# Four feed-forward stages: a 512-column product takes both parts of the operand with the high weights

## The chip, the cores and the metric

The kernel runs on one NeuronCore of one Trainium2 chip. Five engines work side by side, each with its own instruction list: TensorE (PE in the profile; its weight loads are shown apart as PEld), VectorE (DVE), ScalarE (ACT), GpSimd (POOL) and SyncE (SP, which here only issues DMAs). They meet through semaphores. The metric is the device time of one execution in microseconds, and lower is better. Both kernels of this document compute the same function.

## What is computed

The reference is two transformer blocks on 256 tokens with a model width of 1024. The change lies in the feed-forward parts, of which there are four: two with a causal three-tap convolution, and two without it.

```python
def conv_ffn(h, w_up, conv_w, conv_b, w_down):      # stages 0 and 1
    u = h @ w_up                                    # 256x1024 @ 1024x5632
    u = conv(u, conv_w, padding=[(2, 0)], per channel) + conv_b
    a, b = u[..., :D_FF], u[..., D_FF:]             # D_FF = 2816
    return (silu(a) * b) @ w_down                   # 256x2816 @ 2816x1024

def _swiglu(x, w_in, w_out):                        # stages 2 and 3
    gate, up = split(x @ w_in, 2)
    return (silu(gate) * up) @ w_out
```

Each follows `rms_norm(x) * gain`. Around them stand the mixers (a gated linear recurrence, latent attention, memory attention, a convolution with gated linear attention) and an output gate; the change touches none of these.

## The kernel before

**Two parts for every float32 operand.** TensorE multiplies fp32r numbers. For accuracy each operand is split: `w_hi` is the weight rounded to fp32r, `w_lo` the rest, and the activations become `h_hi` and `h_lo` in the same way. `three` (lines 351 to 354) then issues three matmuls into one PSUM region: high by high, high by low, low by high.

**The weight stream.** All weights come as units of 128 x 3072 floats through three slots (`raw`). ScalarE makes `w_hi` of each third of a unit (`hi`, L983), VectorE makes `w_lo` (`lo`, L1502), 1024 columns at a time.

**A feed-forward stage** goes through 22 chunks of 128 hidden channels (`CH = 22`). On TensorE a chunk is `up(j)` and `down(j)`. `up(j)` computes the two halves z = 0 (a) and z = 1 (b) of the chunk: for each half eight contraction steps k, each of them a `three` with 256 columns. Both halves lie side by side in one PSUM bank, `4 + j % 3`, so three chunks are in flight. `down(j)` multiplies the 128 gated channels by the rows of w_down: 12 matmuls of 512 columns into banks 0 to 3, which hold the stage's sum throughout. TensorE's order in the loop is up(j), down(j-2), up(j+1), down(j-1), and so on.

**The evacuation of a chunk** (`body` of ScalarE and of VectorE). VectorE multiplies both halves from PSUM by `rb`, the row factors of the norm, into `tu` (L1604) and signals `tu_done` for each half. In stages 0 and 1 ScalarE starts the convolution (L1078) and VectorE adds the two other taps (L1618). Then come the silu (ScalarE, L1083 or L1086), the product of the halves (VectorE, L1648), and the split of it into `y_hi` and `y_lo` (L983, L1651). Between these steps each engine splits the weights of later units. Instructions of one engine run strictly in the order in which they are written.

**The start of a stage.** `first_up` does chunk 0 while the normed operand still arrives. `spread` then builds the row factors in bank 7 from `late_factors`, ScalarE copies them to `rb`, and TensorE goes on with up(1), up(2), down(0) without a word from VectorE: the only waits of `up` are those for the weights (`s_lo`). Before VectorE's body of chunk 0 stand three weight splits (L1502).

**The end of a stage.** `last_downs` does chunks 20 and 21, and waits with `last_lo_done` for the first half of chunk 21's gated channels; that half comes from the chain tu, convolution, silu, product, y_hi, y_lo (L1604, L1078, L1618, L1083, L1638, L1641).

The names `chain` and `dve_chain` stand for a semaphore on which VectorE waits for results of its own.

Of the kernel before, what the change touches and what calls it, by code (L numbers as in the profile page):

```python
# [17 lines left out]
F32R = mybir.dt.float32r  # L18
# [7 lines left out]
P = 128  # L26
# [105 lines left out]
def build(nc, stream, vectors, masks, x_in, mem_in, pos_in, ple_in, fin_in, out):  # L132
    with ExitStack() as ctx:
# [11 lines left out]
        w_hi = sb("w_hi", [P, SLOTS, UNIT], F32R)  # L145
        w_lo = sb("w_lo", [P, SLOTS, UNIT], F32R)
        x = sb("x", [P, T, D])
        h_hi = sb("h_hi", [P, KT, S], F32R)
        h_lo = sb("h_lo", [P, KT, S], F32R)
        y_hi = sb("y_hi", [P, KT, S], F32R)  # L150
        y_lo = sb("y_lo", [P, KT, S], F32R)
        mem_k = sb("mem_k", [P, 2, 2, S])
# [20 lines left out]
        def A(at, *shape):  # L173
            return room(arena, at, shape)
# [63 lines left out]
        go, gosq = A(0, T, 512), A(1024, T * G_HEADS, P)  # L238
        g_abs = A(8056, T, 256)

        cv, sa, gg, tu = A(0, 3, 512), A(1536, 3, S), A(2304, 3, S), A(6144, 3, 512)

        fin, proj, sg = A(4096, D), A(5120, T, D), A(0, T, D)
# [4 lines left out]
        FFNS = ((U_FFN0, "cw0"), (U_FFN1, "cw1"), (U_FFN2, None), (U_FFN3, None))  # L248
        UP0 = (0, CH, None, None)
        FFN_NORM = (1, 3, 4, 6)  # L250

# [92 lines left out]
        def _(pe):  # L346
# [114 lines left out]
            def ffn(i):  # L461
# [5 lines left out]
                def up_part(j, z, k):  # L467
                    s, a = (U0 + j) % SLOTS, slice(z * PIECE + k * P, z * PIECE + k * P + P)
                    return three(ps[:, 4 + j % 3, z * S:(z + 1) * S], w_hi[:, s, a], w_lo[:, s, a],
                                 h_hi[:, k, :], h_lo[:, k, :], k == 0, k == KT - 1)  # L470

                def up(r, j):
                    for z in range(2):
                        pe.wait_ge(s_lo, lo_at(r, j, z))
                        for k in range(KT):
                            m = up_part(j, z, k)
                    m.then_inc(sem("up_ready"), 1)

                def first_up():
# [499 lines left out]
        def _(act):  # L979
# [83 lines left out]
            def ffn(i):  # L1063
                (U0, cw), n0 = FFNS[i], i * CH

                def at(r, n, per=3):
                    return n if r is None else r * per + n

                def body(r, j):
                    g = j % 3  # L1070
                    if cw:
                        a = _cols[cw][0] + 8 * j

                        def w(n):
                            return vec[:, a + n:a + n + 1] if r is None else vec[:, bass.ds(r * 24 + (a + n), 1)]
                        for z in range(2):
                            act.wait_ge(sem("tu_done"), at(r, 2 * (n0 + j) + z + 1, 6))
                            act.activation(cv[:, g, z * S:(z + 1) * S], tu[:, g, z * S:(z + 1) * S], ACT.Identity,  # L1078
                                           scale=w(4 * z + 2), bias=w(4 * z + 3)).then_inc(sem("ev_done"), 1)
                        if r is not None or j < CH - 1:  # L1080
                            hi(r, U0 + j + 2, 1)
                        act.wait_ge(sem("conv_done"), at(r, n0 + j + 1))
                        act.activation(sa[:, g, :], cv[:, g, 0:S], ACT.Silu).then_inc(sem("silu_done"), 1)  # L1083
                    else:
                        act.wait_ge(sem("tu_done"), at(r, 2 * (n0 + j) + 1, 6))
                        act.activation(sa[:, g, :], tu[:, g, 0:S], ACT.Silu).then_inc(sem("silu_done"), 1)  # L1086
                        if r is not None or j < CH - 1:
                            hi(r, U0 + j + 2, 1)
                    if r is not None or j < CH - 1:
                        hi(r, U0 + j + 2, 2)  # L1090
                    if r is None and j == CH - 1:
                        act.wait_ge(sem("last_gate_done"), i + 1)
                        copy(y_hi[:, g, 0:P], gg[:, g, 0:P]).then_inc(sem("last_hi_done"), 1)
                        act.wait_ge(sem("gate_done"), n0 + CH)
                        copy(y_hi[:, g, P:S], gg[:, g, P:S]).then_inc(sem("g_hi_done"), 1)
                        hi(None, U0 + j + 2, 2)
                        hi(None, U0 + j + 3, 0, up_done=True)
                        return
                    act.wait_ge(sem("gate_done"), at(r, n0 + j + 1))
                    copy(y_hi[:, g, :], gg[:, g, :]).then_inc(sem("g_hi_done"), 1)  # L1100
                    hi(r, U0 + j + 3, 0, up_done=True)
                    if r is None and j == CH - 2:
                        hi(None, U0 + j + 3, 1)

                hi(None, U0 + 2, 0)
                spread(FFN_NORM[i])
                body(None, 0)
                with act.Fori(0, (CH - 1) // 3 - 1) as r:
                    for j in range(1, 4):
                        body(r, j)  # L1110
                for j in range(CH - 3, CH):
                    body(None, j)
# [373 lines left out]
        def _(dve):  # L1486
# [107 lines left out]
            def ffn(i):  # L1594
# [5 lines left out]
                def body(r, j):  # L1600
                    b, g = 4 + j % 3, j % 3
                    dve.wait_ge(sem("up_ready"), at(r, n0 + j + 1))
                    for z in range(2):
                        dve.tensor_tensor(tu[:, g, z * S:(z + 1) * S], ps[:, b, z * S:(z + 1) * S], rb,  # L1604
                                          ALU.mult).then_inc(sem("tu_done"), 1)
                    if cw:
                        marks = []
                        for tap in (1, 0):
# [48 lines left out]
                dve.wait_ge(sem("rb_done"), i + 1)  # L1657
                body(None, 0)
                with dve.Fori(0, (CH - 1) // 3 - 1) as r:
                    chain.enter(r, 9 if cw else 0)  # L1660
                    for j in range(1, 4):
                        body(r, j)
                    chain.leave((CH - 1) // 3 - 1)
# [663 lines left out]
```

## Time and profile before

| | |
|---|---|
| median of 3 runs | 1225.86 us (1224.70 to 1229.43) |
| the profiled execution | 1226.63 us, of which its span is 1224.8 us |
| TensorE matmul busy | 1192.5 us, 8139 matmuls |
| weight loads busy | 1105.2 us |
| VectorE busy | 894.2 us (73%) |
| ScalarE busy | 682.8 us (56%) |
| granted TensorE clock, mean | 0.99 of full |
| DMA | 211.48 MB, mean 173 GB/s |

The profiled execution's time is the span plus 1.83 us around it. A busy TensorE isn't necessarily one at its peak, since matmuls overlap: of two neighbours, start to start is what one costs. The rows below give starts in us from the start of the span. A long uninterrupted stretch of TensorE starts can therefore be counted, and the gaps in it are what other engines cost.

### The profile page before, as it was taken

How to read it: one execution, taken by the hardware profiler on the slowest of the kernel's cores; microseconds unless marked ns; L12 is line 12 of the kernel's file. 1: busy time of each engine (PE TensorE's matmuls, PEld its weight loads, DVE VectorE, ACT ScalarE, POOL GpSimd, SP SyncE). 2: the span in 40 equal slices, each digit the busy share in tenths (PEclk: the TensorE clock that was granted, in tenths of full speed). 3: DMA queues.
4: the chain of work that ended last, by engine and by line, in shares of the span. 5: the costliest groups of instructions: out<-in, count | busy, mean ns of one | idle time of the engine just before them, and what ended most of it. 6: DMA issues, size and time to landing. Idle time of an engine off the chain costs nothing.

```text
span 1224.8 us, 21613 instructions
## 1 busy us (share of the span) xinstructions
PE 1192.5 (97%) x8139; PEld 1105.2 (90%) x8140; DVE 894.2 (73%) x1712; ACT 682.8 (56%) x1206; POOL 3.5 (0%) x9
## 2 busy tenths in 40 slices
PE   9999999999999789999999999999999999999997
PEld 7989979999999667999999999999899889999985
DVE  6987878978778765897877765565789667556566
ACT  6954556655556763665554644443557655444454
POOL 0000000000000000000000000000000000000000
PEclk9999999999999999999999999999999999999998
DMA  9543333554555313365454455545354046554540
GB/s 349 204 177 140 119 138 139 222 193 169 202 181 212 123 53 155 142 220 194 168 203 180 180 214 197 183 176 204 140 184 166 30 165 236 191 191 169 205 155 35
DMA packets 21303, 211.48 MB, mean 173 GB/s; under 512 B 2624, under 2 KB 2880, under 8 KB 4480
## 3 DMA queue, kind: packets, MB, share of 16 engines
q1 hardware_dynamic: 20880, 208.90, 46.3%
q0 software_dynamic: 368, 1.84, 0.4%
q8 instruction: 36, 0.59, 0.2%
q14 instruction: 19, 0.16, 0.0%
HBM read 209.68 MB, written 1.05 MB: 172 GB/s over the span
## 4 chain that ended last, share of the span: by engine, by line
PE 92%; DVE 4%; ACT 3%; issue 1%; POOL 0%; ACTq 0%; POOLq 0%
PE ps L352 28%; PE ps L353 27%; PE ps L354 27%; PE ps L357 8%; ACT arena L983 1%; PE ps L449 1%; DVE h_lo L1584 1%; DVE x L1573 1%; DVE w_lo L1502 1%; ACT w_hi L983 0%; PE ps L593 0%; PE ps L783 0%; DVE arena L1861 0%; DVE arena L1810 0%; DVE arena L1812 0%
## 5 line engine op out<-in xcount | busy, mean ns | idle before, releaser
L1502 DVE TENSOR_TENSOR w_lo<-raw,w_hi 128x1024 fp32r<-128x1024 f32 (+1 forms) x390 | 448.5, 1168 | 71.5 <-ACT w_hi L983 71.2
L352 PE MATMUL ps<-h_hi,w_hi 128*128 128x256 f32 x1608 | 455.8, 283 | 0.0
L353 PE MATMUL ps<-h_lo,w_hi 128*128 128x256 f32 x1608 | 455.0, 283 | 0.0
L354 PE MATMUL ps<-h_hi,w_lo 128*128 128x256 f32 x1608 | 455.0, 283 | 0.0
L983 ACT ACTIVATE w_hi<-raw 128x1024 fp32r<-128x1024 f32 (+1 forms) x390 | 382.9, 1009 | 52.2 <-PE ps L354 48.3
L353 PEld LDWEIGHTS ps<-h_lo,w_hi 128*128 128x128 f32 x1608 | 308.3, 192 | 3.2
L352 PEld LDWEIGHTS ps<-h_hi,w_hi 128*128 128x128 f32 x1608 | 308.3, 192 | 3.2
L354 PEld LDWEIGHTS ps<-h_hi,w_lo 128*128 128x128 f32 x1608 | 308.3, 192 | 0.0
L352 PE MATMUL ps<-w_hi,y_hi 128*128 128x512 f32 (+2 forms) x550 | 211.4, 384 | 1.1 <-DVE y_lo L1872 1.0
L353 PE MATMUL ps<-w_lo,y_hi 128*128 128x512 f32 (+2 forms) x550 | 209.0, 380 | 0.0
L354 PE MATMUL ps<-w_hi,y_lo 128*128 128x512 f32 (+2 forms) x550 | 208.1, 378 | 0.0
L1604 DVE TENSOR_TENSOR arena<-ps,arena 128x256 f32<-128x256 f32 x176 | 66.4, 419 | 108.8 <-PE ps L354 108.8
L352 PEld LDWEIGHTS ps<-w_hi,y_hi 128*128 128x128 f32 x550 | 104.0, 189 | 18.9 <-issue 2.0
L354 PEld LDWEIGHTS ps<-w_hi,y_lo 128*128 128x128 f32 x550 | 103.6, 188 | 19.1
L353 PEld LDWEIGHTS ps<-w_lo,y_hi 128*128 128x128 f32 x550 | 104.0, 189 | 14.7
L1078 ACT ACTIVATE arena<-arena,vec 128x256 f32<-128x256 f32 x88 | 48.2, 594 | 120.3 <-DVE arena L1604 120.3
L1086 ACT ACTIVATE arena<-arena 128x256 f32<-128x256 f32 x44 | 18.4, 418 | 154.0 <-DVE arena L1604 154.0
L1618 DVE SCALAR_TENSOR_TENSOR arena<-arena,vec 128x254 f32<-128x254 f32 (+1 forms) x176 | 77.2, 481 | 25.4 <-ACT arena L1078 25.1
L357 PE MATMUL ps<-arena 128*128 128x64 f32 (+4 forms) x484 | 72.7, 305 | 12.2 <-ACT arena L983 9.5
L357 PEld LDWEIGHTS ps<-arena 128*128 128x128 f32 (+2 forms) x484 | 64.3, 194 | 18.9 <-ACT arena L983 11.0
L352 PE MATMUL ps<-w_hi,h_hi 128*128 128x384 f32 (+3 forms) x208 | 70.1, 337 | 0.0
L354 PE MATMUL ps<-w_hi,h_lo 128*128 128x384 f32 (+3 forms) x208 | 68.8, 331 | 0.0
(272 smaller groups left out, 980.2 us busy)
## 6 DMA issues: line engine op xcount, KB each, us to landing
raw<-in_stream SPq DMA_DIRECT2D x129, 1536.0 KB, 6.5
raw<-in_stream SPq DMA_DIRECT2D x3, 512.0 KB, 6.8
x<-in_x SPq DMA_DIRECT2D x2, 512.0 KB, 4.8
arena<-in_mem SPq DMA_DIRECT2D x1, 1024.0 KB, 13.4
x<-in_x POOLq DMA_DIRECT2D x1, 1024.0 KB, 5.3
out<-arena SPq DMA_DIRECT2D x4, 256.0 KB, 2.1
vec<-in_vectors SPq DMA_DIRECT2D x1, 633.0 KB, 8.1
arena<-in_final POOLq DMA_DIRECT2D x1, 512.0 KB, 3.8
```

Of the source, the lines that this page charges most:

```text
L352: pe.matmul(o, lh, rh, start=start, stop=False, skip_group_check=True)
L353: pe.matmul(o, lh, rl, start=False, stop=False, skip_group_check=True)
L354: return pe.matmul(o, ll, rh, start=False, stop=stop, skip_group_check=True)
L357: return pe.matmul(o, l, r, start=start, stop=stop, skip_group_check=True)
L449: m = pe.transpose(ps[:, XT_BANK[k % 4], (k // 4) * S + t * P:(k // 4) * S + (t + 1) * P], x[:, t, k * P:(k + 1) * P], ident)
L983: return act.activation(o, i, ACT.Copy, scale=scale)
L1078: act.activation(cv[:, g, z * S:(z + 1) * S], tu[:, g, z * S:(z + 1) * S], ACT.Identity, scale=w(4 * z + 2), bias=w(4 * z + 3)).then_inc(s ...
L1086: act.activation(sa[:, g, :], tu[:, g, 0:S], ACT.Silu).then_inc(sem("silu_done"), 1)
L1502: dve.tensor_tensor(w_lo[:, s, a], raw[:, s, a], w_hi[:, s, a], ALU.subtract).then_inc(s_lo, 1)
L1573: dve.scalar_tensor_tensor(x[:, t, r], ps[:, 2 * t + half, :], scale, x[:, t, r], ALU.mult, ALU.add).then_inc(sem("x_done"), 1)
L1604: dve.tensor_tensor(tu[:, g, z * S:(z + 1) * S], ps[:, b, z * S:(z + 1) * S], rb, ALU.mult).then_inc(sem("tu_done"), 1)
L1618: m = dve.scalar_tensor_tensor(c, tu[:, g, z * S:(z + 1) * S - d], w, c, ALU.mult, ALU.add)
```

## The change

Eight rows k of the operand's two parts now lie side by side, so that `h_both[:, k]` is one run of 512 columns. In chunks 1 to 21 of all four stages a step k of a half is no longer three matmuls of 256 columns but two: 512 columns (both parts by `w_hi`), and 256 columns (`h_hi` by `w_lo`) on top of the first half of the result. The sum of a half is then in two pieces that lie in one bank, and someone has to add them: ScalarE copies the second piece to SBUF (`second`), VectorE adds the two from PSUM and SBUF into `tu`, and multiplies by `rb` in place. A half now fills a bank, so the three banks hold three halves and no longer three chunks (`half_bank`), and TensorE waits for `tu_done` ahead of each half. Chunk 0 is computed and evacuated as before.

```diff
+        h_both = sb("h_both", [P, KT, 2, S], F32R)
+        h_hi, h_lo = h_both[:, :, 0, :], h_both[:, :, 1, :]
...
+        def second(i):
+            return cv if FFNS[i][1] is None else A(7680, 3, 512)
...
+        BOTH = (0, 1, 2, 3)
+
+        def half_bank(j, z):
+            return 4 + (2 * j + z + 2) % 3
+
+        def part_at(r, i, j):
+            n = BOTH.index(i) * (CH - 1) + j
+            return n if r is None else r * 3 + n
...
+                def up_both(j, z):
+                    s, b = (U0 + j) % SLOTS, half_bank(j, z)
+                    for k in range(KT):
+                        a = slice(z * PIECE + k * P, z * PIECE + k * P + P)
+                        full(ps[:, b, :], w_hi[:, s, a], h_both[:, k, :, :].rearrange("p a b -> p (a b)"), k == 0, k == KT - 1)
+                        m = full(ps[:, b, 0:S], w_lo[:, s, a], h_hi[:, k, :], False, k == KT - 1)
+                    return m
+
                 def up(r, j):
                     for z in range(2):
                         pe.wait_ge(s_lo, lo_at(r, j, z))
-                        for k in range(KT):
-                            m = up_part(j, z, k)
+                        if i in BOTH:
+
+                            n = max(2 * j + z - 3, 1) + 1 + 2 * n0
+                            pe.wait_ge(sem("tu_done"), n if r is None else r * 6 + n)
+                            m = up_both(j, z)
...
+                        if i in BOTH and (r is not None or j > 0):
+                            act.wait_ge(sem("up_ready"), at(r, n0 + j + 1))
+                            for z in range(2):
+                                m = copy(second(i)[:, g, z * S:(z + 1) * S], ps[:, half_bank(j, z), S:2 * S])
+                            m.then_inc(sem("part_done"), 1)
...
                     dve.wait_ge(sem("up_ready"), at(r, n0 + j + 1))
-                    for z in range(2):
-                        dve.tensor_tensor(tu[:, g, z * S:(z + 1) * S], ps[:, b, z * S:(z + 1) * S], rb,
-                                          ALU.mult).then_inc(sem("tu_done"), 1)
+                    if i in BOTH and (r is not None or j > 0):
+                        sums = []
+                        dve.wait_ge(sem("part_done"), part_at(r, i, j))
+                        for z in range(2):
+                            sums.append(chain.inc(dve.tensor_tensor(tu[:, g, z * S:(z + 1) * S],
+                                                                    ps[:, half_bank(j, z), 0:S],
+                                                                    second(i)[:, g, z * S:(z + 1) * S], ALU.add)))
+                        for z in range(2):
+                            dve.wait_ge(s_chain, chain.at(sums[z]))
+                            v = tu[:, g, z * S:(z + 1) * S]
+                            dve.tensor_tensor(v, v, rb, ALU.mult).then_inc(sem("tu_done"), 1)
```

The copies stand in both branches of ScalarE's `body`. In stages 2 and 3 its second weight piece, `hi(r, U0 + j + 2, 1)`, moves from behind the silu to behind the copies.

The order of instructions changes at two places of interest. The first is TensorE at the start of stage 0, where `spread` (the two rows with `vec,small`) ends and up(1) begins. Before:

```order
L357 MATMUL ps<-zero 128x1 [waits lo_ready]
L357 MATMUL ps<-vec,small 128x128 [waits late_factors]
L357 MATMUL ps<-vec,small 128x128
L352 MATMUL ps<-h_hi,w_hi 128x256 [waits lo_ready]
L353 MATMUL ps<-h_lo,w_hi 128x256
```

And now, where L372 is the matmul of `full`:

```order
L372 MATMUL ps<-zero 128x1 [waits lo_ready]
L372 MATMUL ps<-vec,small 128x128 [waits late_factors]
L372 MATMUL ps<-vec,small 128x128
L372 MATMUL ps<-h_both,w_hi 128x512 [waits tu_done,lo_ready]
L372 MATMUL ps<-h_both,w_lo 128x256
```

The first matmul of up(1) now waits for `tu_done` too; the number is 2, which is both halves of chunk 0. The second place is VectorE's evacuation of a chunk in the loop of stage 0. Before:

```order
L1604 TENSOR_TENSOR arena<-ps,arena 128x256 [waits up_ready]
L1604 TENSOR_TENSOR arena<-ps,arena 128x256
L1615 ISA
L1618 ISA [waits ev_done]
L1618 SCALAR_TENSOR_TENSOR arena<-arena,vec 128x255
```

Now, with the sums (L1649) and the products (L1655):

```order
L1647 REGISTER_ALU [waits up_ready]
L1649 TENSOR_TENSOR arena<-ps,arena 128x256 [waits part_done]
L1649 TENSOR_TENSOR arena<-ps,arena 128x256
L1653 ISA
L1655 TENSOR_TENSOR arena<-arena 128x256 [waits dve_chain]
L1653 REGISTER_ALU
L1655 TENSOR_TENSOR arena<-arena 128x256 [waits dve_chain]
L1669 ISA
```

Two vector instructions have become four, the first behind a wait for ScalarE, the last two behind waits for VectorE's own sums.

## Rows read from the trace of the kernel before

**Rows 1.** The page: busy time, the chain that ended last.
```profile
PE 1192.5 (97%) x8139; PEld 1105.2 (90%) x8140; DVE 894.2 (73%) x1712; ACT 682.8 (56%) x1206; POOL 3.5 (0%) x9
...
PE 92%; DVE 4%; ACT 3%; issue 1%; POOL 0%; ACTq 0%; POOLq 0%
```

**Rows 2.** Timeline (start us, us, what) of TensorE, a steady chunk of stage 0.
```profile
231.00 0.40 PE L352 MATMUL ps<-w_hi,y_hi 128*128 128x512 f32 x1
...
233.75 0.28 PE L352 MATMUL ps<-h_hi,w_hi 128*128 128x256 f32 x1
...
239.50 0.40 PE L352 MATMUL ps<-w_hi,y_hi 128*128 128x512 f32 x1
```

**Rows 3.** Timeline of TensorE: other widths, full clock.
```profile
80.06 0.33 PE L353 MATMUL ps<-w_lo,h_hi 128*128 128x384 f32 x1
80.23 0.33 PE L354 MATMUL ps<-w_hi,h_lo 128*128 128x384 f32 x1
...
867.50 0.39 PE L352 MATMUL ps<-w_hi,y_hi 128*128 128x512 f32 x1
...
871.36 0.39 PE L354 MATMUL ps<-w_hi,y_lo 128*128 128x512 f32 x1
```

**Rows 4.** Timeline of VectorE, one chunk of stage 0, the start before and the next.
```profile
232.84 0.75 DVE L1604 TENSOR_TENSOR arena<-ps,arena 128x256 f32<-128x256 f32 x2
...
239.99 0.75 DVE L1604 TENSOR_TENSOR arena<-ps,arena 128x256 f32<-128x256 f32 x2
241.33 1.77 DVE L1618 SCALAR_TENSOR_TENSOR arena<-arena,vec 128x255 f32<-128x255 f32 x4 [0.59 <-ACT arena L1078]
...
244.15 0.42 DVE L1648 TENSOR_TENSOR arena<-arena 128x256 f32<-128x256 f32 x1
244.49 1.22 DVE L1502 TENSOR_TENSOR w_lo<-raw,w_hi 128x1024 fp32r<-128x1024 f32 x1
...
248.20 0.76 DVE L1604 TENSOR_TENSOR arena<-ps,arena 128x256 f32<-128x256 f32 x2 [0.97 <-PE ps L354]
```

**Rows 5.** Timeline, start of stage 0: spread, up(1), ScalarE's copy, VectorE.
```profile
193.47 0.69 PE L357 MATMUL ps<-vec,small 128*128 128x128 f32 x4
193.91 0.36 PE L352 MATMUL ps<-h_hi,w_hi 128*128 128x256 f32 x1
...
194.19 0.39 ACT L983 ACTIVATE arena<-ps 128x256 f32<-128x256 f32 x1 [0.69 <-PE ps L357]
...
196.23 0.75 DVE L1604 TENSOR_TENSOR arena<-ps,arena 128x256 f32<-128x256 f32 x2
...
204.04 0.75 DVE L1604 TENSOR_TENSOR arena<-ps,arena 128x256 f32<-128x256 f32 x2
```

**Rows 6.** Timeline, start of stage 3: up(1) and VectorE's chunk 0.
```profile
1004.52 0.36 PE L352 MATMUL ps<-h_hi,w_hi 128*128 128x256 f32 x1
...
1006.84 0.75 DVE L1604 TENSOR_TENSOR arena<-ps,arena 128x256 f32<-128x256 f32 x2
```

**Rows 7.** Timeline, end of stage 0: the chain of chunk 21, and TensorE.
```profile
367.20 0.76 DVE L1604 TENSOR_TENSOR arena<-ps,arena 128x256 f32<-128x256 f32 x2 [0.77 <-PE ps L354]
...
370.89 0.29 DVE L1641 TENSOR_TENSOR y_lo<-arena,y_hi 128x128 fp32r<-128x128 f32 x1 [0.18 <-ACT y_hi L983]
...
370.88 0.39 PE L354 MATMUL ps<-w_hi,y_lo 128*128 128x512 f32 x1
371.33 0.47 PE L352 MATMUL ps<-w_hi,y_hi 128*128 128x512 f32 x1
```

**Rows 8.** Timeline of VectorE, end of stage 2.
```profile
865.25 0.29 DVE L1641 TENSOR_TENSOR y_lo<-arena,y_hi 128x128 fp32r<-128x128 f32 x1 [0.17 <-ACT y_hi L983]
```

**Rows 9.** Windows: busy us of PE, PEld, DVE, ACT, POOL, granted clock, DMA.
```profile
145.10:155.00 9.90, 9.23 (x68) 8.96 (x69) 7.00 (x30) 4.78 (x27) 0.44 (x1) 1.00 0.15 62
...
460.80:464.20 3.40, 2.90 (x8) 2.43 (x9) 2.71 (x5) 0.57 (x2) 0.00 (x0) 0.50 0.10 22
```

**Rows 10.** Timeline of TensorE: idle time before, and matmuls at half clock.
```profile
145.02 2.16 PE L357 MATMUL ps<-x,arena 128*128 128x128 f32 x17 [1.08 <-DVE arena L1835]
...
459.37 0.55 PE L812 MATMUL ps<-vec,arena 128*128 128x128 f32 x3 [2.49 <-DVE arena L1999]
...
463.17 0.63 PE L353 MATMUL ps<-w_lo,y_hi 128*128 128x512 f32 x1
463.60 0.63 PE L354 MATMUL ps<-w_hi,y_lo 128*128 128x512 f32 x1
```

More of the change, by code:

```diff
@@ L474, in up @@
                         pe.wait_ge(s_lo, lo_at(r, j, z))
-                        for k in range(KT):
-                            m = up_part(j, z, k)
+                        if i in BOTH:
+                            n = max(2 * j + z - 3, 1) + 1 + 2 * n0
+                            pe.wait_ge(sem("tu_done"), n if r is None else r * 6 + n)
+                            m = up_both(j, z)
+                        else:
+                            for k in range(KT):
+                                m = up_part(j, z, k)
                     m.then_inc(sem("up_ready"), 1)
@@ L1084, in body @@
                     else:
+                        both = i in BOTH and (r is not None or j > 0)
+                        if both:
+                            act.wait_ge(sem("up_ready"), at(r, n0 + j + 1))
+                            for z in range(2):
+                                m = copy(second(i)[:, g, z * S:(z + 1) * S], ps[:, half_bank(j, z), S:2 * S])
+                            m.then_inc(sem("part_done"), 1)
+                            if r is not None or j < CH - 1:
+                                hi(r, U0 + j + 2, 1)
                         act.wait_ge(sem("tu_done"), at(r, 2 * (n0 + j) + 1, 6))
                         act.activation(sa[:, g, :], tu[:, g, 0:S], ACT.Silu).then_inc(sem("silu_done"), 1)
-                        if r is not None or j < CH - 1:
+                        if not both and (r is not None or j < CH - 1):
                             hi(r, U0 + j + 2, 1)
@@ L1602, in body @@
                     dve.wait_ge(sem("up_ready"), at(r, n0 + j + 1))
-                    for z in range(2):
-                        dve.tensor_tensor(tu[:, g, z * S:(z + 1) * S], ps[:, b, z * S:(z + 1) * S], rb,
-                                          ALU.mult).then_inc(sem("tu_done"), 1)
+                    if i in BOTH and (r is not None or j > 0):
[5 more added lines that the diff above has]
+                                                                    second(i)[:, g, z * S:(z + 1) * S], ALU.add)))
+                        for z in range(2):
+                            dve.wait_ge(s_chain, chain.at(sums[z]))
+                            v = tu[:, g, z * S:(z + 1) * S]
+                            dve.tensor_tensor(v, v, rb, ALU.mult).then_inc(sem("tu_done"), 1)
+                    else:
+                        for z in range(2):
+                            dve.tensor_tensor(tu[:, g, z * S:(z + 1) * S], ps[:, b, z * S:(z + 1) * S], rb,
+                                              ALU.mult).then_inc(sem("tu_done"), 1)
                     if cw:
@@ L1659, in ffn @@
                 with dve.Fori(0, (CH - 1) // 3 - 1) as r:
-                    chain.enter(r, 9 if cw else 0)
+                    chain.enter(r, (9 if cw else 0) + (6 if i in BOTH else 0))
                     for j in range(1, 4):
```

2 lines of the change are left out of this document (removed).

## The prediction, made before the changed kernel was run

> **What bounds the kernel now.** I read the page first. Matmuls are busy for 97% of the span and TensorE makes 92% of the chain that ended last [rows 1], so what counts is how long TensorE takes over its list, and every time it stands still. Next the timeline of TensorE over one steady chunk, because a busy TensorE says nothing of its pace. From the first matmul of one down to the first of the next is 239.50 - 231.00 = 8.50 us [rows 2]. Of that, the down's 12 matmuls of 512 columns take 2.75 us (0.229 each), and the up's 48 of 256 columns take 5.75 us (0.120 each). Then the timeline of VectorE, which has the next longest list: when it is behind, a chunk costs it 239.99 - 232.84 = 7.15 us, in which it idles 0.59 us for ScalarE; once it has caught up it idles 0.97 us and more for TensorE [rows 4]. Last, the two ends of a stage, where TensorE could come to wait.
>
> **What the change removes.** Per step k of a half, three matmuls of 256 become one of 512 and one of 256. The columns stay the same, 768; one instruction pair (load and matmul) goes. What is a pair worth? Full clock is 2.4 GHz, so 256 columns stream in 106.7 ns and 512 in 213.3. Start to start it is 120 ns for 256 [rows 2], 170 for 384 (160 streamed), and 3.86 us / 17 = 227 for 512 [rows 3]. So about 13 ns come on top of the streaming, whatever the width. Before a step costs 3 x 120 = 360 ns, after it 227 + 120 = 347. 21 chunks x 4 stages x 16 steps = 1344 steps x 13 ns = **17.5 us** saved. With the down's 229 instead of 227 it is 11 ns, 14.8 us. The round falls from 8.50 to 8.29 us. How a 512 and a 256 alternate the trace doesn't show; the nearest rows are those of each alone, and I take 13 ns with 10 and 26 as ends (26 if the short one lost its whole surplus because its load lies behind the long one).
>
> The Trainium skill ("TensorE: Matmul & The Clock Gate", Back-to-back issue gap) gives an isolated matmul a gap of N / 2.4 + 2.5 ns. By that rule a pair removed would be worth an estimated 2.5 ns, 1344 of them 3.4 us, and the sum would be +16.5 us. The trace does not agree: its three widths show 10 to 14 ns above streaming [rows 2, 3].
>
> **What it adds within a chunk.** ScalarE gets two copies of 128x256 from PSUM. One such copy takes 0.39 us [rows 5], the pair about 0.72. VectorE gets two more operations of 128x256. The two PSUM products take 0.75 us as a pair; an SBUF one costs 244.49 - 244.15 = 0.34 start to start [rows 4]. So four take 0.75 + 0.68 and the body grows by 0.7 us, to 7.15 + 0.7 = 7.85 us. A wait of VectorE on its own first sum is covered by the second sum. 7.85 is below the new 8.29, so VectorE doesn't become the bound of the round: cover 0.44 us. The lower end of the addition is the 0.68 of two more SBUF operations; the upper has ScalarE's copies exposed in every round, 0.68 + 0.77 = 1.45, a body of 8.60, which exceeds 8.29 by 0.31. I take 0.7, because a VectorE that is behind finds the copies done.
>
> The new wait for a bank: the second half of up(j+1) needs the first half of chunk j evacuated. Between the end of up(j) and that point TensorE has a down (2.74) and a half of up (2.78), 5.5 us. The evacuation takes 0.77 (copies and a signal) + 0.69 (sums) + 0.41 = 1.9 us. Hidden, with 3.6 us of cover in the steady state. At up(2) of the start there is no down between, only 2.78 us, and VectorE still has chunk 0's body to finish; worked through below it is met with some 0.3 us to spare. Behind the waiting matmul stands all of TensorE's list, so whatever is not covered counts in full.
>
> **The start of a stage.** This is what speaks against the change. Up(1) used to begin straight behind spread, at 193.91 us in stage 0 [rows 5]. Now its first half waits for `tu_done` 2 + 2 n0, both halves of chunk 0, though it writes banks that chunk 0 doesn't use. VectorE produces them only after three weight splits: 196.23 + 0.75 = 196.98 [rows 5]. Plus some 0.1 us for the signal (371.18 to 371.33 is 0.15 [rows 7]), TensorE stands for 197.1 - 193.91 = 3.2 us. In stage 3 it is 1006.84 + 0.75 + 0.1 - 1004.52 = 3.2 us [rows 6]; stages 1 and 2 have the same lists. Nothing covers it, since TensorE is the bound from there on: 4 x 3.2 = **12.8 us** lost. For up(2): up(1) then ends at 197.1 + 16 x 0.347 = 202.65, the copies are done by 203.7, VectorE comes free at 204.04 [rows 5], its first half is done at 204.04 + 0.69 + 0.41 = 205.15, and TensorE asks at 202.65 + 2.78 = 205.4. No stall, by 0.3 us. The later chunks gain 0.44 us of distance per round.
>
> **The end of a stage.** In stage 0 the chain of chunk 21 starts at 367.20 and delivers at 370.89 + 0.29 = 371.18, and TensorE takes it up at 371.33, 0.45 us behind its last start instead of 0.23, so already late [rows 7]. The chain grows by the copies, 0.77, and the sums, 0.69: 1.46 us, all of it exposed. Two convolution stages: **2.9 us**. In stage 2 the chain delivers at 865.54 [rows 8] and TensorE needs it at 867.50 [rows 3], 1.96 us later; there and in stage 3 the 1.46 is covered.
>
> **The clock.** An idle TensorE can lose its clock. After 2.49 us of idle time [rows 10] came 3.4 us at a granted 0.50, which is 1.2 of 2.4 GHz [rows 9]; after 1.08 us at 145.02 the clock stayed at 1.00 [rows 9, 10]. At half clock 512 columns take 463.60 - 463.17 = 0.43 us instead of 0.227 [rows 10, 3]. In dense work such a stretch loses 3.4 x (1 - 0.227 / 0.43) = 1.6 us. My stalls of 3.2 us are nearer the 2.49 than the 1.08, but they sit in dense work. I take the price as between 0 and 4 x 1.6 = 6.4 us, and choose 70% of it at 1.5 us each, since part of a stretch may fall into the stall: **4.2 us**.
>
> **The sum** against the profiled execution's own 1226.63 us: -17.5 + 12.8 + 2.9 + 4.2 = +2.4, that is 1229.0. That execution is 0.8 us above the median of the runs, so on their scale I forecast 1225.9 + 2.4 = **1228 us**: what the shorter list brings is spent at the starts of the stages. With the ends of the terms: -17.5 + 12.8 + 2.9 + 0 = -1.8 (1224), and -14.8 + 12.8 + 2.9 + 6.4 = +7.3 (1233).
>
> **The rivals.**
> - *The short matmul runs faster behind the long one.* Its load hides behind 213 ns of streaming, and the step costs 334. For it: in the all-256 stretch a load has only 120 ns to hide in. Against it: in the all-512 stretch the load is hidden just as well and the surplus of 13 ns is still there. Saving 26 x 1344 = 35 us: 1226 - 35 + 12.8 + 2.9 + 4.2 = 1211; with half of the extra, 1219. Chance 0.12.
> - *A pair is worth next to nothing* (slower): the surplus isn't paid per instruction but comes back in the mixed stream, say as a wait of the 512 for the load that has only 120 ns of the short one to hide in. Then the step stays at 360 ns and only the costs are left: 1226 + 12.8 + 2.9 + 4.2 = 1246. Against it: a load hidden behind 256 columns is what all of the up has now, at 13 ns. Chance 0.03. The gap rule of the Trainium skill's page named above points the same way.
> - *VectorE becomes the bound of the convolution stages (slower).* The place is the body of chunks 1 to 21 of stages 0 and 1; it decides from a body of 8.29 us on, where mine has 7.85. At 8.60 some 40 rounds cost 0.31 us more each, 12 us: 1240; half way over the edge, 8.45, it is 6 us: 1234. For it: VectorE's margin is the smallest in the kernel, and the copy needs ScalarE first. Against: its 0.97 us of idle time, of which only 0.21 go with the shorter round. Chance 0.10.
> - *The clock falls at every start, and for two stretches* (slower): 4 x 3.2 = 12.8 instead of 4.2: 1237. For it: a stall of 3.2 us may reach into parts of two stretches. Against: the only stretch behind a single gap in the rows is one of 3.4 us. Chance 0.12.
>
> **How the numbers follow.** The main forecast has 0.63, with a range of its own from 1224 to 1233. About what a measurement here can tell from no change is 0.5%, which is 6.1 us: below 1219.7 is faster, above 1232.0 slower. Faster is the first rival, 0.12. Slower are the second, third and most of the fourth, and a sliver of the main case: 0.22. The same is left with 0.66. The range, 1221 to 1236, holds the main case, part of the fourth rival and the milder half of the third, and leaves out the faster rival and the dear ends.
>
> **What would show it.** In the changed profile: a step k of 0.347 us start to start, and rounds of 8.29 us between first downs. At each of four stage starts an idle time of about 3.2 us of TensorE, released by VectorE's second product of chunk 0, and behind most of them a granted clock of 0.50 for 3.4 us. At 371 us, less what was shifted, a TensorE gap 1.5 us longer than before in stages 0 and 1, none in 2 and 3. In the convolution stages VectorE still idle before its sums. The prediction fails if the step costs under 0.340 us or VectorE has no idle time left there.

## The result, and the profile after

| | before | after |
|---|---|---|
| median of the runs | 1227.64 us (4 runs) | 1239.22 us (4 runs, 1238.13 to 1242.98) |
| ratio after / before | | 1.0092, 95% interval 1.0069 to 1.0116 |
| profiled execution, span | 1224.8 us | 1236.9 us |
| matmuls | 8139 | 6796 |

The kernel became slower by 0.9%, some 11 us, where 1228 and "no change" were forecast, with a range that ended at 1236. 1343 matmuls are gone, as they should be. The page after (section 1, then section 4, the chain that ended last), against [rows 1]:

```profile
PE 1189.7 (96%) x6796; PEld 1039.1 (84%) x6796; DVE 947.3 (77%) x1880; ACT 736.8 (60%) x1374; POOL 3.5 (0%) x9
...
PE 87%; DVE 8%; ACT 3%; issue 1%; DMA 0%; SPq 0%; DVEq 0%; ACTq 0%
```

TensorE's share of the chain fell from 92 to 87% and VectorE's doubled from 4 to 8%: TensorE now stands and waits for VectorE. The view of who waited for whom (total us, times, longest) names where:

```profile
PE ps L372 <- DVE arena L1658: 11.9, 4, 3.0
...
PE ps L367 <- DVE y_lo L1695: 3.0, 2, 1.5
```

L1658 is the product of chunk 0 with `rb`, once in each of four stages. L1695 is the last chunk's `y_lo`, once in each of stages 0 and 1. Neither row is among the waits of the kernel before.

**A round.** The timeline of TensorE over the round that answers to [rows 2], from the first matmul of one down to that of the next:

```profile
242.00 0.40 PE L367 MATMUL ps<-w_hi,y_hi 128*128 128x512 f32 x1
...
244.75 0.39 PE L372 MATMUL ps<-h_both,w_hi 128*128 128x512 f32 x1
244.97 0.28 PE L372 MATMUL ps<-h_both,w_lo 128*128 128x256 f32 x1
245.09 0.40 PE L372 MATMUL ps<-h_both,w_hi 128*128 128x512 f32 x1
245.32 0.28 PE L372 MATMUL ps<-h_both,w_lo 128*128 128x256 f32 x1
245.44 0.40 PE L372 MATMUL ps<-h_both,w_hi 128*128 128x512 f32 x1
245.68 0.28 PE L372 MATMUL ps<-h_both,w_lo 128*128 128x256 f32 x1
245.80 0.40 PE L372 MATMUL ps<-h_both,w_hi 128*128 128x512 f32 x1
...
250.39 0.40 PE L367 MATMUL ps<-w_hi,y_hi 128*128 128x512 f32 x1
```

The round takes 250.39 - 242.00 = 8.39 us and not 8.29, and nothing in it stands. The up's 16 steps take 250.39 - 244.75 = 5.64 us, 352.5 ns each where 347 were forecast: the 512 that follows a 256 costs 0.23 to 0.24 (mean 0.236) and not 0.227, and the 256 behind it 0.117.

**VectorE in a round**, against [rows 4]:

```profile
249.65 1.22 DVE L1544 TENSOR_TENSOR w_lo<-raw,w_hi 128x1024 fp32r<-128x1024 f32 x1
251.28 0.76 DVE L1649 TENSOR_TENSOR arena<-ps,arena 128x256 f32<-128x256 f32 x2 [0.41 <-ACT arena L1012]
251.95 0.75 DVE L1655 TENSOR_TENSOR arena<-arena 128x256 f32<-128x256 f32 x2
253.39 1.75 DVE L1672 SCALAR_TENSOR_TENSOR arena<-arena,vec 128x255 f32<-128x255 f32 x4 [0.69 <-ACT arena L1112]
```

It still idles 0.41 us before its sums, where 0.97 stood. It isn't the bound.

**The start of a stage**, against [rows 5] (timeline of TensorE, stage 0):

```profile
191.87 0.69 PE L372 MATMUL ps<-vec,small 128*128 128x128 f32 x4
195.52 0.56 PE L372 MATMUL ps<-h_both,w_hi 128*128 128x512 f32 x1 [2.96 <-DVE arena L1658]
...
196.73 0.63 PE L372 MATMUL ps<-h_both,w_hi 128*128 128x512 f32 x1
197.15 0.42 PE L372 MATMUL ps<-h_both,w_lo 128*128 128x256 f32 x1
197.37 0.63 PE L372 MATMUL ps<-h_both,w_hi 128*128 128x512 f32 x1
...
199.24 0.39 PE L372 MATMUL ps<-h_both,w_hi 128*128 128x512 f32 x1
199.47 0.28 PE L372 MATMUL ps<-h_both,w_lo 128*128 128x256 f32 x1
```

After 2.96 us of idle time up(1) begins, and at first a step takes 197.37 - 196.73 = 0.64 us instead of 0.35. The windows behind three of the starts (stages 0, 1, 2; busy us of each engine, then the granted clock, the DMA share and GB/s) say why:

```profile
195.80:199.20 3.40, 3.40 (x12) 2.84 (x11) 3.06 (x6) 3.37 (x5) 0.00 (x0) 0.50 0.88 372
...
506.40:513.20 6.80, 5.97 (x19) 5.13 (x20) 5.66 (x12) 5.94 (x8) 0.00 (x0) 0.50 0.63 233
702.40:709.00 6.60, 6.55 (x37) 5.75 (x38) 4.22 (x5) 3.92 (x8) 0.00 (x0) 1.00 0.74 284
```

Half clock for 3.4 us in stage 0 and for 6.8 us in stage 1, none in stage 2 after the same standing, and 3.4 us in stage 3. A granted clock of 0.50 is 1.2 of 2.4 GHz.

**The end of stage 0**, against [rows 7]:

```profile
371.68 0.39 PE L369 MATMUL ps<-w_hi,y_lo 128*128 128x512 f32 x1
373.55 0.47 PE L367 MATMUL ps<-w_hi,y_hi 128*128 128x512 f32 x1 [1.48 <-DVE y_lo L1695]
```

The gap from start to start grew from 0.45 to 1.87 us.

**The bill**, from starts of TensorE's list in the two traces. The mark is the one-column matmul at the end of `first_up`; from it to the first down it took 12.07 us in every stage before, and 16.59, 17.75, 15.08 and 16.44 us after, in which 3.21 us are standing (from the mark to up(1) it is 3.70 instead of 0.49) and 0.23 are saved in two ups (in the bill, that 0.23 is part of the shorter rounds).

| term | forecast | measured |
|---|---|---|
| shorter rounds, 84 chunks | -17.5 | 84 x (8.387 - 8.500) = -9.5 |
| standing at four starts | +12.8 | 4 x 3.21 = +12.8 |
| half clock behind the starts | +4.2 | 1.54 + 2.70 + 0.03 + 1.39 = +5.7 |
| two late ends | +2.9 | 2 x 1.42 = +2.8 |
| everything outside the feed-forward stages | 0 | +0.2 |
| sum | +2.4 | +12.0 (spans: +12.1) |

The +0.2 is luck and not calm. Ahead of stage 0 the changed kernel was 1.6 us faster, and a stretch of 3.4 us of half clock at 75.1 us in the trace before is absent from its own; in the mixer between stages 0 and 1 it was 1.7 us slower, with 20.5 us of half clock in all instead of 13.7. No edit touches either place. With one traced execution of each kernel, terms of 1 to 2 us outside the stages can't be put down to the change.

### The profile page after: what moved, and what is told of

It is laid out like the page before. It is cut to its first block, busy times and chain, and to the rows that moved or that the text cites. A ratio compares the mean times of both kernels' runs of the same rounds, so it can differ in the third digit from the quotient of the medians.

```text
span 1236.9 us, 19658 instructions
## 1 busy us (share of the span) xinstructions
PE 1189.7 (96%) x6796; PEld 1039.1 (84%) x6796; DVE 947.3 (77%) x1880; ACT 736.8 (60%) x1374; POOL 3.5 (0%) x9
## 4 chain that ended last, share of the span: by engine, by line
PE 87%; DVE 8%; ACT 3%; issue 1%; DMA 0%; SPq 0%; DVEq 0%; ACTq 0%
PE ps L372 45%; PE ps L367 13%; PE ps L368 13%; PE ps L369 13%; DVE w_lo L1544 2%; DVE h_both L1626 1%; ACT arena L1012 1%; PE ps L464 1%; ACT w_hi L1012 1%; DVE x L1615 1%; DMA x<-in_x 0%; DVE arena L1672 0%; ACT h_both L1012 0%; PE ps L812 0%; PE ps L622 0%
## 5 line engine op out<-in xcount | busy, mean ns | idle before, releaser
L372 PE MATMUL ps<-h_both,w_hi 128*128 128x512 f32 x1344 | 483.4, 402 | 11.9 <-DVE arena L1658 11.9
L372 PE MATMUL ps<-h_both,w_lo 128*128 128x256 f32 x1344 | 380.2, 283 | 0.0
L372 PEld LDWEIGHTS ps<-h_both,w_hi 128*128 128x128 f32 x1344 | 255.7, 190 | 74.7 <-DVE w_lo L1544 12.5
L372 PEld LDWEIGHTS ps<-h_both,w_lo 128*128 128x128 f32 x1344 | 257.0, 191 | 2.9
L1012 ACT ACTIVATE arena<-ps 128x256 f32<-128x256 f32 (+3 forms) x201 | 69.2, 394 | 183.7 <-PE ps L372 172.8
L1649 DVE TENSOR_TENSOR arena<-ps,arena 128x256 f32<-128x256 f32 x168 | 63.4, 419 | 120.2 <-ACT arena L1012 120.1
L372 PE MATMUL ps<-arena 128*128 128x64 f32 (+4 forms) x484 | 73.0, 306 | 12.4 <-ACT arena L1012 9.7
L372 PEld LDWEIGHTS ps<-arena 128*128 128x128 f32 (+2 forms) x484 | 64.6, 195 | 19.0 <-ACT arena L1012 11.0
L367 PE MATMUL ps<-h_both,w_hi 128*128 128x256 f32 x264 | 75.6, 287 | 0.0
L368 PE MATMUL ps<-h_both,w_hi 128*128 128x256 f32 x264 | 74.8, 283 | 0.0
L369 PE MATMUL ps<-h_both,w_lo 128*128 128x256 f32 x264 | 74.7, 283 | 0.0
L367 PE MATMUL ps<-w_hi,h_both 128*128 128x384 f32 (+3 forms) x208 | 69.5, 334 | 0.0
```

The lines of the kernel that those rows point to most:

```text
L367: pe.matmul(o, lh, rh, start=start, stop=False, skip_group_check=True)
L368: pe.matmul(o, lh, rl, start=False, stop=False, skip_group_check=True)
L369: return pe.matmul(o, ll, rh, start=False, stop=stop, skip_group_check=True)
L372: return pe.matmul(o, l, r, start=start, stop=stop, skip_group_check=True)
L1012: return act.activation(o, i, ACT.Copy, scale=scale)
L1649: sums.append(chain.inc(dve.tensor_tensor(tu[:, g, z * S:(z + 1) * S], ps[:, half_bank(j, z), 0:S], second(i)[:, g, z * S:(z + 1) * S], AL ...
```

## The experiments

"Both repairs" below is runs of two and no wait at up(1). All ratios are to the kernel before, run on the same chip between them. The kernel before was slower by 2 to 3 us on these chips than its 1227.64, so the ratios are what to compare. Two rows whose intervals overlap are not told apart by their times; there the traces, in which a round or a start can be read to 0.01 us, carry the argument.

| kernel | median us | ratio (95% interval) |
|---|---|---|
| after | 1239.22 | 1.0092 (1.0069 to 1.0116) |
| runs of eight | 1236.76 | 1.0056 (1.0035 to 1.0078) |
| runs of two (one execution) | 1233.99 | |
| no wait at up(1) | 1234.06 | 1.0025 (1.0010 to 1.0040) |
| before plus the wait | 1249.02 | 1.0152 (1.0124 to 1.0181) |
| both repairs | 1226.97 | 0.9982 (0.9960 to 1.0003) |
| both repairs, stages 2 and 3 alone | 1221.39 | 0.9947 (0.9928 to 0.9967) |
| both repairs, stages 0 and 1 alone | 1235.34 | 1.0051 (1.0035 to 1.0068) |
| both repairs, chunk 21 old | 1223.56 | 0.9962 (0.9946 to 0.9978) |
| after with a fill | 1234.49 | 1.0057 (1.0031 to 1.0082) |
| both repairs, chunk 21 old, fill | 1223.67 | 0.9957 (0.9935 to 0.9979) |

### What a step costs: the order of the two widths

```diff
-                    for k in range(KT):
-                        a = slice(z * PIECE + k * P, z * PIECE + k * P + P)
-                        full(ps[:, b, :], w_hi[:, s, a], h_both[:, k, :, :].rearrange("p a b -> p (a b)"), k == 0, k == KT - 1)
-                        m = full(ps[:, b, 0:S], w_lo[:, s, a], h_hi[:, k, :], False, k == KT - 1)
+                    for g in range(0, KT, RUN):
+                        for k in range(g, g + RUN):
+                            a = slice(z * PIECE + k * P, z * PIECE + k * P + P)
+                            full(ps[:, b, :], w_hi[:, s, a], h_both[:, k, :, :].rearrange("p a b -> p (a b)"), k == 0, k == KT - 1)
+                        for k in range(g, g + RUN):
+                            a = slice(z * PIECE + k * P, z * PIECE + k * P + P)
+                            m = full(ps[:, b, 0:S], w_lo[:, s, a], h_hi[:, k, :], False, k == KT - 1)
```

With RUN = 8:

> The changed kernel with the order within a half of up altered alone: first the eight 512-column products, then the eight 256-column ones (all the waits, copies and sums stay). Theory M (a step costs 353 ns because widths alternate; each width alone costs 227 and 120): a step falls to 347 to 348 ns, the round of a chunk from 8.39 to 8.29 or 8.30 us, the kernel by 84 x 0.09 = 8 us against the changed one, to about 1231. Rival W (a 512-column product from h_both costs 233 ns in itself, by its operand or its place in the loop): step and round stay at 353 ns and 8.39 us, time 1239. Rival V (the round is held by VectorE or ScalarE): the round stays at 8.39 and PE shows gaps.

And RUN = 2:

> As the one with runs of eight, but in runs of two: 512, 512, 256, 256. Theory M with a price per change of width: half as many changes, so half of the excess of 6 ns per step goes: 350 ns, round 8.34 us, about 4 us under the changed kernel. Rival W: 353 ns and 8.39 us as before. If the excess needs a longer run of one width to go, the step stays nearer 353.

The rounds are 8.307 us with runs of eight and 8.293 us with runs of two, in all four stages, against 8.387 in turn. The timeline of TensorE with runs of eight shows one up and the start of its down; here x8 is eight matmuls in one row:

```profile
245.64 1.98 PE L373 MATMUL ps<-h_both,w_hi 128*128 128x512 f32 x8
247.45 1.12 PE L373 MATMUL ps<-h_both,w_lo 128*128 128x256 f32 x8
248.40 2.00 PE L373 MATMUL ps<-h_both,w_hi 128*128 128x512 f32 x8
250.25 1.11 PE L373 MATMUL ps<-h_both,w_lo 128*128 128x256 f32 x8
251.20 0.40 PE L368 MATMUL ps<-w_hi,y_hi 128*128 128x512 f32 x1
```

An up takes 251.20 - 245.64 = 5.56 us, 347.5 ns per step. The first eight 512-column products stand behind a down's products of the same width and cost 1.81 / 8 = 0.226 each; the eight at 248.40 come behind 256-column ones and cost 1.85 / 8 = 0.231. So it is the order that costs, and the theory that a product from `h_both` is dear in itself falls: same operands, same waits, another order, and the step is at the forecast 347. (The whole kernel gained 4.4 us by its ratio, and not 8, and the two intervals overlap: the rounds give 84 x 0.08 = 6.7, and the profiled execution has 0.9 us more at the starts, 2.9 us more ahead of stage 0, where it ran at half clock for 6.8 us and the changed kernel didn't, and 1.2 us more in the mixer behind stage 0.) What doesn't hold is my price per change of width. A run of two has many more changes than a run of eight and is as short (5.563 us per up, with 0.017 less in the down). The excess is on the single alternation. In the mean of 76 rounds the 512s of the changed kernel that follow a 256 cost 232 to 241 ns and the 256s 113 to 120; in runs of two a pair of 512s costs 233 + 231 or 236, and the two 256s behind it 113 + 119 or 116 + 113. Why a second 256 wins back what the first 512 lost, the trace doesn't tell.

### The wait at the start of a stage

The wait taken away, its banks being free:

```diff
-                            pe.wait_ge(sem("tu_done"), n if r is None else r * 6 + n)
+                            if j > 1:
+                                pe.wait_ge(sem("tu_done"), n if r is None else r * 6 + n)
```

> The changed kernel without the wait for tu_done ahead of up(1), alone; its two halves go into banks that nothing holds. Theory S (each stage start costs TensorE 3.24 us of standing, and the clock falls behind three of four): up(1) starts straight behind spread; the wait moves to the second half of up(2), which needs VectorE's first half of chunk 1. In stages 2 and 3 that is about 1.0 us instead of 3.24, in stages 0 and 1 still about 2.8 us, since VectorE's list ahead of it is as long. Sum -5.4 us, and with no fall of the clock in stages 2 and 3 another -1.5: about 1232. Rival: the wait is only brought forward and VectorE's lateness sets all four starts: no more than -2 us, 1237.

From the mark to the first down: 16.14, 16.08, 12.87 and 12.90 us. In stages 2 and 3 that is 0.8 above the kernel before, with the 0.23 saved a standing of 1.0 us, as expected. In stages 0 and 1 the wait moved to the second half of up(2), with 2.65 us of idle time (the row is stage 0's), and the clock fell behind both:

```profile
206.11 0.77 PE L372 MATMUL ps<-h_both,w_hi 128*128 128x512 f32 x1 [2.65 <-DVE arena L1656]
...
205.80:209.20 3.40, 3.09 (x9) 2.67 (x10) 2.71 (x7) 2.86 (x5) 0.00 (x0) 0.50 0.91 390
519.80:523.20 3.40, 3.40 (x12) 2.87 (x11) 3.40 (x7) 2.78 (x5) 0.00 (x0) 0.50 0.48 205
700.40:717.00 16.60, 15.78 (x89) 13.42 (x88) 15.50 (x24) 11.17 (x19) 0.00 (x0) 1.00 0.68 243
```

The last window is the whole start of stage 2, at full clock. The ratio went from 1.0092 to 1.0025, 8 us: the theory of the standing is right, and it has two causes, a needless wait in all stages and VectorE's list in stages 0 and 1.

The wait put into the kernel before, without anything else:

```diff
+                pe.wait_ge(sem("tu_done"), 2 + 2 * n0)
                 up(None, 1)
                 up(None, 2)
```

> The kernel before with one thing added: TensorE waits for both halves of chunk 0 (tu_done) ahead of up(1) in all four stages. Nothing else of the change is in it. Theory S: 4 x 3.2 us of standing, and 1.5 to 3 us of clock behind most of them: +12.8 + 4 to 7, about 1243 to 1246 against 1226. If the clock took no part: 1239. Rival (the standing is made up for later, by work that was waiting anyway): below 1235.

It costs 1.5%, 18.7 us of 1230, inside the 16.8 to 19.8 us that were expected. From the mark to the first down it took 17.75, 17.92, 16.70 and 16.62 us: 4 x 3.11 us of standing and 5.7 + 5.8 + 4.6 + 4.6 - 12.4 = 8.3 us of half clock, which here came behind all four starts. (The spans differ by 23.6 us; the other 2.9 are again more half clock ahead of stage 0 and behind it.) This is the experiment that isolates the largest loss of the change: the rest of the change has no part in it.

### The clock, taken apart from the standing

```diff
+                            if r is None and j == 1 and z == 0:
+                                warm(13, ps[:, 5, :])
                             pe.wait_ge(sem("tu_done"), n if r is None else r * 6 + n)
```

> The changed kernel, with 13 matmuls of zeros (bf16, 512 columns, 0.218 us each) into bank 5 ahead of the wait at up(1), so that TensorE works while it waits; they add nothing to the result. Theory C (behind a standing of 3.2 us the clock falls to 0.50, and that costs 1.5 to 2.8 us each time): no half clock behind the four starts, and from the mark at the end of first_up to the first down 12.07 + 3.2 - 0.23 = 15.0 us in all four stages instead of 16.6, 17.8, 15.1 and 16.4: about -5.5 us against the changed kernel, ratio to before 1.005. Rival (the clock falls there for another reason, or the fill delays up(1)): 16 us and more, ratio 1.009.

Four times 15.00 or 15.01 us, as forecast, and at full clock throughout the four starts, the first and the third of them here:

```profile
195.00:212.00 17.00, 16.95 (x91) 13.18 (x89) 15.16 (x27) 11.99 (x20) 0.00 (x0) 1.00 0.51 186
...
696.20:713.00 16.80, 16.76 (x90) 12.99 (x88) 14.23 (x24) 10.39 (x17) 0.00 (x0) 1.00 0.60 219
```

The ratio fell from 1.0092 to 1.0057, 4.3 us, with intervals that overlap; the four starts in the traces are 5.85 us shorter in sum. One execution with four clean starts could be luck, since the changed kernel had one clean start itself. But of the sixteen starts with a standing of 3.1 or 3.2 us and no fill in the four traced kernels (after, runs of eight, runs of two, before plus the wait) thirteen have half clock behind them, seven of 3.4 us and six of 6.8 us, and of the four with the fill none. So a standing of 3.2 us costs 3.2 us, and what follows it is the clock's, which useless work prevents.

### Both repairs, and where the new form pays

> The changed kernel with both repairs: products in runs of two (512, 512, 256, 256) and no wait ahead of up(1). If the terms add: rounds of 8.29 us (84 x 0.207 = -17.4 against the kernel before), stage starts of +2.8 in stages 0 and 1 and +0.85 in 2 and 3 (+7.3), one stretch of half clock behind each of the two long ones (+3), stage ends +2.9: -4.2 us against before, ratio 0.9966. Rival (VectorE, now with less room in the convolution stages, holds the round there): rounds of stages 0 and 1 above 8.29, ratio 1.00 or more.

The rounds are 8.293 us in all four stages, so VectorE doesn't hold the convolution stages even with the shorter round; the rival falls. The ratio is 0.9982, half of the expected gain, and its interval holds 1, so no gain is shown. From the mark to the first down it took 17.10 and 16.09 us in stages 0 and 1 (6.8 and 3.4 us of half clock), and 12.88 and 12.87 in the others; the mixer behind stage 0 took 3.0 us more than in the kernel before, with 20.5 us of half clock. The edits of the next two are the line `BOTH = (2, 3)` and the line `BOTH = (0, 1)`.

> Both repairs, and the new form in stages 2 and 3 alone; stages 0 and 1 are computed as before. If the terms add: 42 x 0.207 = -8.7, two starts at +0.85, no fall of the clock, no late stage end: -7.0 us against before, ratio 0.9943, the best of all. Rival (what a stage gains is lost elsewhere, so the number of changed stages decides): half of what both repairs bring in all four stages, ratio 0.998.

> Both repairs, and the new form in stages 0 and 1 alone. If the terms add: -8.7 of rounds, two starts at +2.8, two stretches of half clock +3, two late ends +2.9: +2.8 us against before, ratio 1.0023. Rival as for the kernel with stages 2 and 3 alone: ratio 0.998.

Stages 2 and 3 alone: 0.9947 (expected 0.9943), the lowest ratio of the study and clear of the kernel before, though not of the two kernels with chunk 21 old. Stages 0 and 1 alone: 1.0051, slower, with 16.27 and 16.20 us at their starts and 1.89 us gaps at their ends. That is 3.4 us worse than the 1.0023 expected, and the trace doesn't say why: its execution took 1231.18 us, 4.5 us more than that of the kernel before, which the starts, rounds and ends (+3.3) and the stretches outside them (+1.2) account for, while the median of its runs is 1235.34. In both kernels the rounds of the changed stages are 8.293 us and those of the others 8.500. The saving per chunk is the same in both kinds of stage; what differs are the start and the end. It isn't the number of changed stages that decides. TensorE's waits in the kernel with stages 2 and 3 alone (us in total, times, longest) show what is left:

```profile
PE ps L373 <- DVE arena L1660: 1.8, 2, 0.9
```

### The end of a convolution stage

```diff
+        def is_both(i, r, j):
+            return r is not None or (j > 0 and not (i < 2 and j == CH - 1))
...
-                            m = up_both(j, z)
+                            if is_both(i, r, j):
+                                m = up_both(j, z)
+                            else:
+                                for k in range(KT):
+                                    a = slice(z * PIECE + k * P, z * PIECE + k * P + P)
+                                    t = (U0 + j) % SLOTS
+                                    m = three(ps[:, half_bank(j, 0), z * S:(z + 1) * S], w_hi[:, t, a], w_lo[:, t, a],
+                                              h_hi[:, k, :], h_lo[:, k, :], k == 0, k == KT - 1)
```

The two halves of chunk 21 lie in one bank again, so TensorE waits ahead of the first of them alone.

> Both repairs in all four stages, and chunk 21 of stages 0 and 1 in the old form (three matmuls of 256, no copy, no sum), so that the chain at the stage's end has its old length. Theory E (each late end is the 1.46 us of copies and sums on that chain): the gap of TensorE before the last chunk's down falls from 1.87 us to some 0.45 us in both stages, for 2 x 0.2 us of up: -2.5 us against the same kernel with chunk 21 in the new form, ratio 0.9945. Rival (the late end comes from VectorE being behind in these stages): the gap stays above 1 us and the time the same.

```profile
371.20 0.39 PE L373 MATMUL ps<-w_hi,y_lo 128*128 128x512 f32 x1
372.22 0.47 PE L371 MATMUL ps<-w_hi,y_hi 128*128 128x512 f32 x1 [0.64 <-DVE y_lo L1710]
```

The gap is 1.02 us: less than the 1.89 of the same form with a new chunk 21, more than the 0.45 of before. Both theories have a share. The 1.46 us of copies and sums leave the chain, but in this kernel VectorE comes to chunk 21 late, straight out of a weight split. Its list from chunk 20's sums on, with the same place in the kernel before as the last row:

```profile
359.80 0.76 DVE L1664 TENSOR_TENSOR arena<-ps,arena 128x256 f32<-128x256 f32 x2 [1.76 <-ACT arena L1027]
...
365.83 2.35 DVE L1559 TENSOR_TENSOR w_lo<-raw,w_hi 128x1024 fp32r<-128x1024 f32 x2
368.10 0.75 DVE L1673 TENSOR_TENSOR arena<-ps,arena 128x256 f32<-128x256 f32 x2
...
358.70 0.76 DVE L1604 TENSOR_TENSOR arena<-ps,arena 128x256 f32<-128x256 f32 x2 [2.63 <-PE ps L354]
```

It begins without idle time, where before it had idled 0.77 [rows 7]. Chunk 20's body still has copies and sums, and the starts add up. Before, VectorE began chunk 20 at 358.70, 0.20 us behind the first matmul of the down that follows its up (358.50), and now at 359.80, 0.97 behind (358.83): 0.77 for the copies. From there to chunk 21 it was busy 367.20 - 358.70 - 0.77 = 7.73 us, and now 368.10 - 359.80 = 8.30: 0.57 for the sums. Of these 1.34 us the old idle time takes 0.77, and 0.57 are left, which is the growth of the gap from 0.45 to 1.02. So with a new chunk 21 two things end together, VectorE's list and the chain of copies and sums, and either alone would make TensorE late. In the whole time the gain is not clear of noise (0.9962 against 0.9982, intervals that overlap, 0.9945 expected).

Last, the same kernel with a fill at its two remaining long standings:

```diff
+                            if i < 2 and r is None and j == 2 and z == 1:
+                                pe.wait_ge(sem("rb_done"), i + 1)
+                                warm(12)
```

> Both repairs in all four stages, chunk 21 of stages 0 and 1 in the old form, and 12 matmuls of zeros into bank 7 ahead of the second half of up(2) in stages 0 and 1, where TensorE still stands for 3.03 us. Theory C: the two stretches of half clock behind these starts go, from the mark to the first down 16.2 becomes 14.7 us: -3 us against the same kernel without the fill (ratio 0.9962), so ratio 0.9938, level with the kernel that has the new form in stages 2 and 3 alone. Rival: the same 16.2 us and 0.996.

From the mark to the first down: 14.67 and 14.65 us, as expected, at full clock. The ratio, 0.9957 against 0.9962 and an expected 0.9938, doesn't show it; its runs spread from 1217.87 to 1227.94. In the profiled one the half clock shows elsewhere, in the mixer between stages 0 and 1:

```profile
426.20:450.10 23.90, 20.18 (x79) 16.46 (x80) 10.97 (x29) 10.02 (x31) 0.00 (x0) 0.50 0.18 66
```

It does so once more for 6.8 us from 467.2 on. There the kernel with stages 2 and 3 alone and the same kernel without the fill had 10.2, 3.4 and 3.4 us, with full clock between, and the mixer took 6.7 us less. No edit touches this stretch.

## Why the prediction was wrong

**The shorter list: the step that failed.** The prediction put a step at 227 + 120 = 347 ns by adding two widths, each read from a long stretch of its own kind, and took "13 ns with 10 and 26 as ends". A step measured 352.5, and the one before, by its rounds, 5.753 / 16 = 359.6, so a pair is worth 7.1 ns: 1344 of them -9.5 us instead of -17.5. That one term is 8.0 of the 9.6 us between the two sums of the bill. With it alone put right the forecast would have been 1236, the very end of the range; 1.5 us of clock and a kernel before whose median came out 1.8 us higher make up the rest of the way to 1239. Runs of eight and of two (347.4 and 347.7) show that the sum was right for widths that don't alternate singly. The rows held a warning that I named and passed over: a down took 0.229 per matmul and the long stretch 0.227. It is the 512s just behind the 256s of an up that are dear, 233, 236, 228, 233 and 231 ns in the mean of the kernel before, then 227: the price of a mix, in the trace of before. The low end should have been a step with this 233, 353, close to what was measured, though there the 512s are dearer (236) and the 256s cheaper (117). The 170 ns that I read for 384 columns came from rounded starts; the long stretch gives 173, 13 ns above streaming like the other widths. The rival that the surplus "comes back in the mixed stream" was right that the mix costs and wrong in size (nothing left, where 7.1 ns are), and stood at 0.03 because I tested it against uniform stretches. Its reason, a 512 that waits for its weight load, was not tested: what makes the single alternation dear stays open.

**The standing at the starts: right.** 3.2 us forecast, 3.21 measured, in all four; the wait alone, put into the kernel before, shows it.

**The clock: right in kind, small in size.** 4.2 forecast, 5.7 measured. The rival of two stretches came true in one of four starts. With the wait alone it was 8.3.

**The ends: the size right, the reason half.** 2.9 forecast, 2.8 measured, none in stages 2 and 3. The forecast put all of it on chunk 21's own chain; the run with an old chunk 21 shows that VectorE's list behind chunk 20 would have made TensorE 0.57 us late by itself.

**VectorE as the bound of the convolution stages: rightly held unlikely.** A body of 7.85 us forecast, and 7.85 between its starts while it is behind; a cover of 0.44 us forecast, 0.41 of idle time measured, if in a round of 8.39; with rounds of 8.293 it still doesn't bound.

**Up(2) with 0.3 us to spare: right.** The kernel with the fill has stages 0 and 1 at full clock, and its 15.00 us there are 12.07 + 3.2 - 0.23, which leaves no second standing.

**The range.** Each term but one was inside its ends. The range took in the clock's ends and not a pair worth less than 11 ns (even the 10 named as an end was not carried into it); it also stood on a median of 1225.86, where the four runs beside the changed kernel gave 1227.64. And it gave nothing to the clock outside the stages, which moved by 1.6 and 1.7 us here and cancelled.

## What to carry to other kernels

Fewer, wider matmuls with the same columns bring only the surplus per instruction, here 12 ns of 120, and alternating widths one by one gave 5 of them back: run at least two of a width in a row. When a region is made twice as large, count what the smaller number in flight makes the producer wait for at the start and the end of a loop, where no other work lies between, before counting the steady round, and write each wait for what the bank really held. Where a standing can't be avoided and is near 3 us, filling it with useless matmuls saved the half clock behind it, here 1.5, 2.7, 0 and 1.4 us at four starts. It didn't show in the time of the one kernel that was already at 0.996, whose clock fell for longer elsewhere.

## What the runs showed of the hardware that was not expected

- A 512-column fp32r matmul behind a 256-column one costs 232 to 241 ns from start to start, in a run of its own 227; a 256 behind a 512 costs 113 to 120 and in its own run 120. Two and two in turn average 347.7 ns per pair, as runs of eight do (347.4); one and one 352.5.
- The same standing of 3.2 us was followed by 0, 3.4 or 6.8 us of half clock in the four starts of one execution (over four kernels: three, seven and six starts of sixteen), and one of 2.64 to 2.76 us (the four kernels with the new form in stages 0 and 1, no wait at up(1) and no fill) by 3.4 us in seven of eight starts and by 6.8 in one. Behind the fill, in six starts of two kernels, there was none.
- The half clock in the mixer between stages 0 and 1 varied between kernels whose instructions there are the same: its longest stretch from 10.2 to 23.9 us, its sum from 13.7 to 30.7. It is the likely cause of the spread of about 10 us between runs of one kernel, but only one execution of each was traced, so that was not shown.
